# First norm taken from token rows, constants loaded between weight chunks, output turned by diagonal products and stored tile by tile

## The chip, the cores and the metric

One core of one Trainium2 chip runs the whole program. The metric is device time in microseconds (us) of one execution; the lower, the better. Engines: PE is TensorE, DVE is VectorE, ACT is ScalarE, POOL is GpSimd, SP is SyncE, which here only issues DMAs. Three runs of the kernel before gave 3411.03 us in the median (3408.16 to 3412.96).

## The reference

512 tokens of 1024 features, float32, pass two stacks of two layers each.

```python
def first_block(x, ...):
    for l in range(2):
        h = rmsnorm(x, mix_norm[l])
        p = h @ w_in[l]                       # 1440 columns
        a = mla_mixer(p..., positions, ...)   # 8 heads, with rotated positions
        b = pool_mixer(p..., w_pool[l], pool_scale[l])
        c = sg_mixer(p..., sg_norm[l], w_s[l], b_s[l])
        x = x + concat(a, b, c) @ w_o[l]
        h = rmsnorm(x, ffn_norm[l])
        x = x + (silu(h @ w_gate[l]) * (h @ w_up[l])) @ w_down[l]
    return rmsnorm(x, final_norm)

def second_block(x, c, ctx, c_ctx, ...):      # also 256 context tokens
    for l in range(2):
        sh1, sc1, g1, sh2, sc2, g2 = ada_params(c, ada_w[l], ada_b[l])
        y = mixer(rmsnorm_2(x, norm_g[l, 0]) * (1 + sc1) + sh1, ...)
        x = x + g1 * rmsnorm_2(y, norm_g[l, 1])
        h = rmsnorm_2(x, norm_g[l, 2]) * (1 + sc2) + sh2
        x = x + g2 * rmsnorm_2(swiglu(h, ...), norm_g[l, 3])
    return x
```

A norm divides each token's features by the root of the mean of their squares and multiplies them by a gain per feature.

## The kernel before

**Layout.** Activations lie transposed: xT is [128 features, 8 groups k, 512 tokens]. The input arrives as token rows (xin, four tiles of 128 tokens, 512 KB each) and PE turns it into xT by 32 transposes against an identity; the output is turned back in the same way (L3510), copied from PSUM to xout by ACT and DVE (L1400, L2499), and stored by one DMA (L645).

**Products in three parts.** A float32 matrix is split into a high part (rounded, "H") and the remainder ("L"), and each product is H·H + H·L + L·H. For a chunk c of weights, SP loads raw[c % 2] (L491), ACT makes WH (`hi(c)`, L728) once PE has used chunk c-2, and POOL makes WL (`low_parts`, L675). PE waits for WL (`chunk(c)`), SP for the WL of chunk c-2 before it loads over the raw buffer. A chunk of the first projection is 48 products of 512 columns.

**Norms.** ACT squares each group, the squares are added (by DVE, L1428, for the norms in ADDED; by PE, L2575, for the others), PE sums over partitions (L2587), ACT takes the root (L746), DVE the reciprocal (L1435), and PE spreads it over partitions with four products against the identity (L2603, `to_all`) into M[1]. Then, for each k, DVE makes ht = x · gain · M[1] (L1458), ACT rounds it to hH (L782, `rounded`), DVE makes hL = ht - hH (L1450), and PE multiplies as they come (`opening`, L2536). `rounded` lets ACT make one weight chunk's high part (`late`) after k = 1. In stages named in AWAKE, `keep_busy` sends products of the identity with itself into S[0] (L2565) where PE would idle; "b0.n1", the first norm, is not among them.

**Start.** Queues run in program order:

- SP: four tiles of x (L606), chunks 0 and 1, then `small_operands` (L547 to L555: 38 DMAs of constants, most of them 4 bytes for each element, all counted by the semaphore consts_loaded), then chunk 2 and the rest.
- ACT: `hi(0)`, `hi(1)`, half of the copies from PSUM to xT (L1086), the squares, the root, the rounding; then it waits for consts_loaded, takes Silu of cvec (L820), Exp of lbe (L822) and Sin for the rotation tables (L824), and goes on to the latents (L831) and `hi(2)`.
- DVE: the other half of the copies (L1744), the sums, the norm, then `once()`: the bounds (L1665 to L1681) and the angles (L1687 to L1703).
- PE: the 32 transposes, the norm's sums, chunks 0, 1, 2 and so on (`first_mixing`).

**End.** The last feed-forward adds its products to m_y (L1528). Then comes the norm "m.y2" and, in `added`, for each k: ht = m_y · gain · M[1] (L2074) and xT = xT + ht (L2081); then the transposes.

**The norm m.n2**, ahead of the last feed-forward, is one of those that PE sums (`column_sums`, L2575, with one product of `keep_busy` between two k).

## Time and profile before

| | |
|---|---|
| median of 3 runs | 3411.03 us (3408.16 to 3412.96) |
| the profiled execution | 3414.15 us, its span 3412.3 us |
| PE busy | 3179.8 us (93%) |
| DVE, ACT, POOL busy | 1898.6, 1149.3, 1242.3 us |
| chain that ended last, by engine | PE 77%, DVE 14%, ACT 4% |
| mean granted clock of PE | 0.957 |

The times inside the trace count from the start of the span. An engine's row "[11.17 <-POOL WL L675]" says that the engine sat idle for 11.17 us before this instruction, and that POOL's instruction of line 675 ended that. "x8" is the number of instructions merged; a float32 product against the identity or the ones counts as two matmul records, a transpose as one. PEclk is the granted clock of PE: 1.00 is 2.4 GHz, 0.50 is 1.2 GHz.

### The profile page before, as it was taken

The page shows a single profiled execution, that of the slowest core. Times are in us where ns is not written, and L with a number is a line of the kernel's source. Part 1 is how long each engine was busy: PE and PEld are TensorE (multiplying, and loading weights), DVE is VectorE, ACT ScalarE, POOL GpSimd, SP SyncE. Part 2 cuts the span into 40 slices and gives each one's busy share as a digit, 9 for nine tenths or more (in the row PEclk, how much of TensorE's full clock was granted, in tenths as well). Part 3 has the DMA queues.
Part 4 walks back from the last instruction along what each step waited for, and adds up shares of the span by engine and source line. Part 5 has one row for each costly group of instructions (what it writes and reads, how often), then busy time and mean ns, then how long its engine had stood idle before and what let it go on. Part 6 is the DMA issues. An engine that isn't in the chain of part 4 may idle for free.

```text
span 3412.3 us, 41861 instructions
## 1 busy us (share of the span) xinstructions
PE 3179.8 (93%) x16574; PEld 2612.2 (77%) x16574; DVE 1898.6 (56%) x3031; ACT 1149.3 (34%) x1801; POOL 1242.3 (36%) x556
## 2 busy tenths in 40 slices
PE   5888999998899999998999989889999999999997
PEld 4646788877469888777888988768888876788886
DVE  2753778766644454674434867558665437352224
ACT  3343222233435432324335544332223324432221
POOL 2301444533027543334344445124444330134442
PEclk8889999999899999998999989789999899999998
DMA  6201355533025332223333333125554220113331
GB/s 116 68 13 50 124 176 155 167 100 75 18 70 152 114 89 82 74 75 99 99 101 100 108 102 118 62 75 173 169 171 130 69 75 1 38 56 102 96 93 50
DMA packets 481716, 324.41 MB, mean 95 GB/s; under 512 B 103617, under 2 KB 448833, under 8 KB 481009
## 3 DMA queue, kind: packets, MB, share of 16 engines
q1 hardware_dynamic: 477056, 310.37, 30.9%
q10 hardware_dynamic: 2656, 6.30, 0.5%
q0 software_dynamic: 1808, 5.05, 0.5%
q8 instruction: 132, 2.16, 0.3%
q14 instruction: 64, 0.52, 0.0%
HBM read 316.41 MB, written 5.24 MB: 94 GB/s over the span
## 4 chain that ended last, share of the span: by engine, by line
PE 77%; DVE 14%; ACT 4%; issue 2%; SPq 2%; POOL 1%; DVEq 0%; DMA 0%; ACTq 0%
PE G L2511 11%; PE G L2520 11%; PE G L2521 11%; PE G L2525 11%; PE G L2695 5%; PE G L2696 5%; PE G L2700 5%; PE G L2536 2%; PE M L2875 2%; POOL WL L675 1%; PE S L2511 1%; PE M L2575 1%; ACT WH L728 1%; SPq L555 1%; DVE rstd L1428 1%
## 5 line engine op out<-in xcount | busy, mean ns | idle before, releaser
L675 POOL TENSOR_TENSOR WL<-raw,WH 128x1024 fp32r<-128x1024 f32 (+1 forms) x520 | 1225.5, 2379 | 2029.4 <-ACT WH L728 2029.4
L728 ACT ACTIVATE WH<-raw 128x1024 fp32r<-128x1024 f32 (+1 forms) x520 | 492.6, 995 | 625.4 <-PE G L2700 415.3
L2520 PE MATMUL G<-hH,WH 128*128 128x512 f32 x1520 | 595.6, 392 | 0.0
L2521 PE MATMUL G<-hL,WH 128*128 128x512 f32 x1520 | 592.8, 390 | 0.0
L2525 PE MATMUL G<-hH,WL 128*128 128x512 f32 x1520 | 360.1, 389 | 0.0
L2520 PEld LDWEIGHTS G<-hH,WH 128*128 128x128 f32 x1520 | 285.9, 188 | 60.2
L2521 PEld LDWEIGHTS G<-hL,WH 128*128 128x128 f32 x1520 | 285.9, 188 | 58.9
L2525 PEld LDWEIGHTS G<-hH,WL 128*128 128x128 f32 x1520 | 285.3, 188 | 59.3
L1491 DVE SCALAR_TENSOR_TENSOR acc<-adaw,cvec,acc 128x512 f32<-128x512 f32 x280 | 250.6, 947 | 4.2
L2511 PE MATMUL G<-hH,WH 128*128 128x512 f32 (+1 forms) x448 | 177.3, 396 | 29.5 <-POOL WL L675 26.9
L2511 PE MATMUL G<-hH,WL 128*128 128x512 f32 (+1 forms) x448 | 173.7, 388 | 0.0
L2511 PE MATMUL G<-hL,WH 128*128 128x512 f32 (+1 forms) x448 | 173.6, 388 | 0.0
L1515 DVE TENSOR_TENSOR FH<-silu,G 128x512 fp32r<-128x512 f32 x44 | 30.2, 687 | 215.6 <-PE G L2525 158.3
L2695 PE MATMUL G<-FH,WH 128*128 128x512 f32 x352 | 142.2, 404 | 0.2 <-DVE xT L1528 0.2
L2696 PE MATMUL G<-FL,WH 128*128 128x512 f32 x352 | 140.1, 398 | 0.0
L1428 DVE TENSOR_TENSOR rstd<-rstd,sq 128x512 f32<-128x512 f32 (+1 forms) x105 | 76.2, 725 | 104.0 <-ACT sq L763 96.8
L2511 PEld LDWEIGHTS G<-hH,WH 128*128 128x128 f32 x448 | 87.7, 196 | 48.5 <-POOL WL L675 28.2
L792 ACT ACTIVATE silu<-G 128x512 f32<-128x512 f32 x44 | 26.3, 598 | 273.2 <-PE G L2525 264.4
L1518 DVE TENSOR_TENSOR FL<-silu,FH 128x512 fp32r<-128x512 f32 x44 | 107.5, 2444 | 1.5
L1515 DVE TENSOR_TENSOR m_FH<-m_silu,G 128x512 fp32r<-128x512 f32 x22 | 15.1, 687 | 158.6 <-PE G L2525 156.3
L2511 PEld LDWEIGHTS G<-hL,WH 128*128 128x128 f32 x448 | 87.8, 196 | 16.5 <-issue 0.7
L2511 PEld LDWEIGHTS G<-hH,WL 128*128 128x128 f32 x448 | 87.4, 195 | 16.8
(659 smaller groups left out, 6338.0 us busy)
## 6 DMA issues: line engine op xcount, KB each, us to landing
raw<-ffn_w_in_in SPq DMA_DIRECT2D x264, 256.0 KB, 3.4
adaw<-ada_w_in SPq DMA_DIRECT2D x48, 1024.0 KB, 5.3
raw<-ab_w_in_in SPq DMA_DIRECT2D x128, 256.0 KB, 3.0
raw<-ffn_w_out_in SPq DMA_DIRECT2D x96, 256.0 KB, 2.9
raw<-w_gate_in SPq DMA_DIRECT2D x88, 256.0 KB, 3.4
raw<-w_up_in SPq DMA_DIRECT2D x88, 256.0 KB, 3.5
raw<-w_down_in SPq DMA_DIRECT2D x64, 256.0 KB, 2.8
raw<-w_in_in SPq DMA_DIRECT2D x40, 256.0 KB, 3.1
```

The lines of the kernel that those rows point to most:

```text
L675: nc.gpsimd.tensor_tensor(WL[c % 2][:, cut], raw[c % 2][:, cut], WH[c % 2][:, cut].bitcast(F32), ALU.subtract)\
L728: nc.scalar.activation(WH[c % 2][:, cut], raw[c % 2][:, cut], ACT.Copy).then_inc(weights_hi, 1)
L1428: V.tensor_tensor(rstd[:, 0:cols], rstd[:, 0:cols], sq[:, k % 2, 0:cols], ALU.add).then_inc(dve_done, did("dve", f"{n}.ad{k}"))
L1491: V.scalar_tensor_tensor(sums[:, b, i, :], weights[h % 2][:, k, :], col, sums[:, b, i, :], ALU.mult, ALU.add)\
L1518: V.tensor_tensor(FL[:, j, :], silu[:, t % 2, :], FH[:, j, :].bitcast(F32), ALU.subtract).then_inc(dve_done, did("dve", f"{n}.FL{t}"))
L2511: last = mm(dst, x, y, start=(k == 0 and j == 0), stop=(k == K - 1 and j == 2))
L2520: mm(dst, view(WH[c % 2], k), high, start=(k == 0 and not (joint and i)), stop=False)
L2521: mm(dst, view(WH[c % 2], k), low, start=False, stop=False)
L2525: last = mm(dst, view(WL[c % 2], k), X(k)[0], start=False, stop=(k == K - 1 and not (joint and i == 0)))
L2695: mm(dst, part(WH, k, cols, o), high, start=(k == 0 and not (joint and i)), stop=False)
L2696: mm(dst, part(WH, k, cols, o), low, start=False, stop=False)
L2700: last = mm(dst, part(WL, k, cols, o), X(k)[0], start=False, stop=(k == count - 1 and not (joint and i == 0)))
```

## The change

- The four tiles of x have a semaphore each. As each tile lands, ACT squares its token rows with the sum accumulated along the row (no sums on DVE or PE), and PE transposes its 8 blocks; ACT and DVE copy them to xT. The root is taken from the four sums; PE only spreads it. "b0.n1" joins AWAKE, and PE sends 8 products of the identity ahead of each tile.
- ACT makes `hi(0)` after the root and `hi(1)` as `late` in the rounding. PE starts the opening with half of chunk 0's low part.
- Six constants (rope_cols, posi, g_q, g_kv) are issued by ACT's queue. The others stand on SP's queue between chunks 1, 2, 3, 4 and 5, with three semaphores in place of one. `once()` is split: the angles stay behind the first norm, the bounds, Silu and Exp go behind the first attention.
- The norm m.n2 has, for each k, four transposes of xT in place of one `keep_busy` product; ACT copies them to xtok, in token rows.
- The tail: gdiag[k] = identity · gain (8 DVE instructions inside the last feed-forward). PE makes m_y (as left operand) times gdiag into eight half tiles in eight PSUM banks, and DVE adds each, times the token's 1/root, to xtok in one instruction. Each tile is stored as it is ready. The 16 DVE instructions of `added`, the spreading, and the eight copies to xout are gone.

```diff
-        CONSTS = 2 + 4 * DEPTH + 2 + 2 + 6 * DEPTH + 6 + 3 + 3
+        CONSTS = DEPTH + 1 + 2 + 6 * DEPTH + 6 + 3 + 3
+        TURNS = 2 + 2 * DEPTH
+        POOLING = 1 + DEPTH
...
                 if l == 0:
-                    small_operands()
+                    small_operands_0()
...
                 for n in range(3):
+                    if l == 0:
+                        (small_operands_1, small_operands_2, small_operands_3)[n]()
                     load(c + 3 + n, columns(c + 3 + n, w, r0 + ROPE + n * 2 * P))
...
-            sp.dma_start(out[0].rearrange("(t p) d -> p t d", p=P), xout[:, :, :]).then_inc(stored, 16)
+            for t in range(4):
+                sp.wait_ge(dve_done, at("dve", f"out.{t}1"))
+                sp.dma_start(out[0, t * P:t * P + P, :], xtok[:, t, :]).then_inc(stored, 16)
...
+            for t in range(4):
+                act.wait_ge(x_loaded[t], 16)
...
+                nc.scalar.activation(spare..., xin[:, t, :], ACT.Square, accum_out=rstd[:, t:t + 1])
+                act.wait_ge(pe_done, at("pe", f"x.{t}"))
+                nc.scalar.activation(xT[:, 0:4, t * P:t * P + P], G[2 * (t % 2)][:, :]..., ACT.Copy)
+            act.wait_ge(act_done, here())
+            nc.scalar.activation(rstd[:, 4:8], rstd[:, 0:4], ACT.Sqrt, bias=eps[:, 0:1], scale=1.0 / D)
             hi(0)
-            hi(1)
...
+            pe.wait_ge(early_loaded, 16)
+            for t in range(4):
+                keep_busy("b0.n1", 8)
+                pe.wait_ge(x_loaded[t], 16)
...
+                for k in range(KD):
+                    last = nc.tensor.transpose(G[2 * (t % 2) + k // 4][...], xin[:, t, k * P:k * P + P], ident[:, :])
+                last.then_inc(pe_done, did("pe", f"x.{t}"))
+            keep_busy("b0.n1", 8)
...
+            pe.wait_ge(dve_done, at("dve", f"gdiag{KD - 1}"))
+            for t in range(2):
+                out_blocks(t, range(KD - 2))
+            pe.wait_ge(dve_done, at("dve", f"m.down3.{KD - 1}"))
+            for t in range(2):
+                out_blocks(t, range(KD - 2, KD))
+            pe.wait_ge(dve_done, at("dve", f"m.y2.ad{KD - 1}"))
...
+            out_blocks(2, range(KD))
+            out_blocks(3, range(4))
+            pe.wait_ge(dve_done, at("dve", "m.y2.rec"))
+            out_blocks(3, range(4, KD))
```

SP's queue at the start, from chunk 1 on (raw_52 holds even chunks, raw_53 odd ones; every x counts DMAs). Before:

```order
L491 DMA raw_53<-w_in_in 128x2x256 x4
L547 DMA pool_inv<-tables_in 128x1024
L550 DMA g_ffn<-ffn_norm_in 128x8x1 x2
L552 DMA posi<-positions_in 128x512
L555 DMA ada_b<-ada_b_in 128x48x1 x2
L555 DMA g_n<-norm_g_in 128x8x1 x4
L555 DMA lbe<-hgrn_lb_in 128x4x1 x6
L555 DMA gate_b<-ab_gate_b_in 16x1
L491 DMA raw_52<-w_in_in 128x8x128
```

and in the change:

```order
L497 DMA raw_53<-w_in_in 128x2x256 x4
L549 DMA g_pool<-pool_scale_in 128x2x1 x2
L549 DMA g_ffn<-ffn_norm_in 128x8x1 x2
L497 DMA raw_52<-w_in_in 128x8x128 [waits weights_lo]
L565 DMA pool_inv<-tables_in 128x1024
L549 DMA ada_b<-ada_b_in 128x48x1 x2
L549 DMA lbe<-hgrn_lb_in 128x4x1 x6
L497 DMA raw_53<-w_in_in 128x2x256 [waits weights_lo]
L549 DMA g_n<-norm_g_in 128x8x1 x4
L497 DMA raw_52<-w_in_in 128x2x256 [waits weights_lo]
L549 DMA gate_b<-ab_gate_b_in 16x1
```

Of the 38 small DMAs that stood ahead of chunk 2, 7 still do; 9 now stand between chunks 2 and 3, 4 between 3 and 4, 12 between 4 and 5, and 6 are on ACT's queue.

PE at the start (S is the bank that `keep_busy` writes, M<-ident,ncol the spreading, L2536 and L2606 the opening). Before:

```order
L2887 MATMUL G<-ident,xin 128x128 x32
L2587 MATMUL M<-ones,rstd 128x1 x4
L2603 MATMUL M<-ident,ncol 128x128 x4
L2536 MATMUL G<-hH,WH_54 128x512
L2536 MATMUL G<-hL,WH_54 128x512
```

and in the change, where the first two rows come four times:

```order
L2637 MATMUL S<-ident 128x128 x8
L2980 MATMUL G<-ident,xin 128x128 x8
L2637 MATMUL S<-ident 128x128 x10
L2688 MATMUL M<-ident,ncol 128x128 x4
L2606 MATMUL G<-hH,WH_54 128x512
L2606 MATMUL G<-hL,WH_54 128x512
```

The sums over partitions are gone, and 42 products of the identity stand between the transposes and ahead of the spreading.

PE at the end, behind the last product of the feed-forward. Before:

```order
L2700 MATMUL G<-m_FH,WL_57 128x512 x8
L2565 MATMUL S<-ident 128x128 x8
L2587 MATMUL M<-ones,rstd 128x1 x4
L2565 MATMUL S<-ident 128x128 x2
L2603 MATMUL M<-ident,ncol 128x128 x4
L3510 MATMUL G<-ident,xT 128x128 x32
```

and in the change:

```order
L2785 MATMUL G<-m_FH,WL_57 128x512 x8
L3602 MATMUL G<-gdiag,m_y_244 128x128 x6
L3602 MATMUL S<-gdiag,m_y_244 128x128 x6
L3602 MATMUL S<-gdiag,m_y_244 128x128 x2
L3614 MATMUL M<-ones,rstd 128x1 x4
L3602 MATMUL M<-gdiag,m_y_244 128x128 x4
L3602 MATMUL G<-gdiag,m_y_244 128x128 x8
```

Sixteen of the 32 diagonal products stand ahead of the sums, and nothing is spread or transposed behind them.

## Rows read from the trace of the kernel before

**Rows 1.** Timeline of PE from the start: start us, us, instruction, count, idle before.

```profile
11.48 3.68 PE L2887 MATMUL G<-ident,xin 128*128 128x128 f32 x16 [11.48 <-DMA xin<-x_in]
...
32.73 2.08 PE L2603 MATMUL M<-ident,ncol 128*128 128x128 f32 x8 [0.55 <-DVE ncol L1435]
...
71.68 0.80 PE L2511 MATMUL G<-hH,WH 128*128 128x512 f32 x1 [11.17 <-POOL WL L675]
```

**Rows 2.** Timeline of SP's queue, DMA issues.

```profile
10.61 1.41 SPq L547 DMA_DIRECT2D pool_inv<-tables_in  x1
...
23.97 5.52 SPq L555 DMA_DIRECT2D ada_b<-ada_b_in  x2
29.54 6.37 SPq L555 DMA_DIRECT2D g_n<-norm_g_in  x4
...
47.23 4.56 SPq L555 DMA_DIRECT2D lbe<-hgrn_lb_in  x6
...
55.18 22.00 SPq L491 DMA_DIRECT2D raw<-w_in_in  x16
```

**Rows 3.** Timelines of DVE and POOL, end of the first norm and the angles.

```profile
44.60 1.48 DVE L1450 TENSOR_TENSOR hL<-ht,hH 128x512 fp32r<-128x512 f32 x2
...
59.68 0.42 DVE L1687 CAST posf<-posi 64x512 f32<-64x512 int32 x1
...
66.96 9.30 POOL L675 TENSOR_TENSOR WL<-raw,WH 128x1024 fp32r<-128x1024 f32 x4 [43.12 <-ACT WH L728]
```

**Rows 4.** Tile xin: landing. Tile ident: issue (ns, first and last start) and landing.

```profile
DMA to landing us min/median/max: 3.7/6.6/9.3
...
L652 POOL DMA_DIRECT2D ident<-tables_in x1: 679/679/679, 1.2 to 1.2; - x1
...
DMA to landing us min/median/max: 6.1/6.1/6.1
```

**Rows 5.** Timeline of PE around the norms of the last layer.

```profile
2984.48 1.95 PE L2565 MATMUL S<-ident 128*128 128x128 f32 x16
...
2998.58 1.71 PE L2575 MATMUL M<-ones,sq 128*128 128x1 f32 x8
...
3007.54 1.91 PE L2603 MATMUL M<-ident,ncol 128*128 128x128 f32 x8
```

**Rows 6.** Timelines of DVE and POOL in the norm b0.n2.

```profile
337.94 1.53 DVE L1458 SCALAR_TENSOR_TENSOR ht<-xT,g_ffn,M 128x512 f32<-128x512 f32 x2 [1.25 <-PE M L2603]
...
344.97 2.09 DVE L1450 TENSOR_TENSOR hL<-ht,hH 128x512 fp32r<-128x512 f32 x1
...
350.52 1.47 DVE L1450 TENSOR_TENSOR hL<-ht,hH 128x512 fp32r<-128x512 f32 x2
...
341.16 5.35 POOL L675 TENSOR_TENSOR WL<-raw,WH 128x1024 fp32r<-128x1024 f32 x2 [12.75 <-ACT WH L728]
```

**Rows 7.** A stretch of PE at full clock: us, PE busy (records), PEclk, DMA share, GB/s.

```profile
49.40:60.40 11.00, 11.00 (x50) 1.00 0.70 95
```

**Rows 8.** The chain that ended last, behind the wait at 71.68 us.

```profile
71.68 19.38 PE G L2511 x72
```

**Rows 9.** The output's transposes: weight loads in ns, and PE by stretch, as in rows 7.

```profile
L3510 PEld LDWEIGHTS G<-ident,xT x32: 139/144/230, 3399.3 to 3404.1; 128*128 128x128 f32 x32
...
3400.00:3402.00 2.00, 2.00 (x11) 0.50 0.03 8
3402.00:3404.00 2.00, 2.00 (x18) 0.97 0.00 0
```

**Rows 10.** Timelines of DVE and SP at the end.

```profile
3380.30 3.07 DVE L1428 TENSOR_TENSOR rstd<-rstd,sq 128x512 f32<-128x512 f32 x4
...
3387.20 0.75 DVE L2074 SCALAR_TENSOR_TENSOR ht<-m_y,mcols,M 128x512 f32<-128x512 f32 x1 [2.17 <-PE M L2603]
...
3398.53 0.69 DVE L2081 TENSOR_TENSOR xT<-xT,ht 128x512 f32<-128x512 f32 x1
...
3405.26 0.40 SPq L645 DMA_DIRECT2D out<-xout  x1
```

More of the change, by code:

```diff
@@ L1095, in _ @@
                     hi(c + 3)
+                    act.wait_ge(consts_loaded, 16 * CONSTS)
+                    nc.scalar.activation(cvec[:, :, :], cvec[:, :, :], ACT.Silu).then_inc(act_done, did("act", "cvec"))
+                    act.wait_ge(dve_done, at("dve", "lb.x"))
+                    nc.scalar.activation(lbe[:, :, :, :], lbe[:, :, :, :], ACT.Exp).then_inc(act_done, did("act", "lb.e"))
                     for k in range(4):
@@ L1397, in _ @@
             second_half(PM, xT)
-            for t in range(4):
-                act.wait_ge(pe_done, at("pe", f"out.{t}"))
-                nc.scalar.activation(xout[:, t, 0:512], G[2 * (t % 2)][:, :], ACT.Copy).then_inc(act_done, did("act", f"out.{t}"))
         @block.vector
@@ L2089, in second_half @@
                 feed_forward(n, ps.y2, N, ps.FH, ps.FL, ps.silu, fresh=True, between=between, last=f"{n}.y2")
-                added(n, 2, ps.y2, x, gain(p, 3), N)
+                if n == "m":
+                    added_sums("m.y2")
+                    roots("m.y2")
+                    for t in range(4):
+                        for half in range(2):
+                            dve.wait_ge(pe_done, at("pe", f"out.{t}{half}"))
+                            dve.wait_ge(dve_done, here())
+                            o = xtok[:, t, half * 512:half * 512 + 512]
+                            V.scalar_tensor_tensor(o, OUT[t][half][:, :], ncol[:, t:t + 1], o, ALU.mult, ALU.add).then_inc(dve_done, did("dve", f"out.{t}{half}"))
+                else:
+                    added(n, 2, ps.y2, x, gain(p, 3), N)
             def own(ins, name):
@@ L2495, in _, with last_gains @@
             added("m", 1, j_y, xT, gain("m", 1), T)
-            second_half(PM, xT, "m")
-            for t in range(4):
-                dve.wait_ge(pe_done, at("pe", f"out.{t}"))
-                V.tensor_copy(xout[:, t, 512:1024], G[2 * (t % 2) + 1][:, :]).then_inc(dve_done, did("dve", f"out.{t}"))
+            def last_gains():
+                for k in range(KD):
+                    yield
+                    V.tensor_scalar(gdiag[:, k, :], ident[:, :], gain("m", 3)(k), None, ALU.mult).then_inc(dve_done, did("dve", f"gdiag{k}"))
+            second_half(PM, xT, "m", last_gains())
         @block.tensor
@@ L2540, in came @@
             def came(n, k):
+                if n == "b0.n1" and k == KD // 2:
+                    pe.wait_ge(weights_lo, 2)
                 pe.wait_ge(act_done, at("act", f"{n}.H{k}"))
@@ L2588, in feature_sums @@
                     last.then_inc(pe_done, did("pe", f"{n}.sum"))
+                elif n == "m.n2":
+                    for k in range(K):
+                        pe.wait_ge(act_done, at("act", f"m.n2.sq{k}"))
+                        for t in range(4):
+                            last = mm(M[0][:, t:t + 1], sq[:, k % 2, t * P:t * P + P], ones[:, 0:1], start=(k == 0 and t == 0), stop=(k == K - 1 and t == 3))
+                        last.then_inc(pe_done, did("pe", f"m.n2.sq{k}"))
+                        if k == K - 1:
+                            tally.also("pe", "m.n2.sum")
+                        if k >= 4:
+                            pe.wait_ge(act_done, at("act", f"m.xt{k - 4}"))
+                        for t in range(4):
+                            last = nc.tensor.transpose(G[k % 4][:, t * P:t * P + P], xT[:, k, t * P:t * P + P], ident[:, :])
+                        last.then_inc(pe_done, did("pe", f"m.xt{k}"))
                 else:
```

168 lines of the change are left out of this document (105 added, 63 removed).

## The prediction

> **What bounds the kernel now.** The page comes first: PE is busy for 93% of the span and holds 77% of the chain that ended last, so a change pays only where PE stands still or runs at its low clock. The change touches three such places, so I read the timelines of the first 100 us, of the norm m.n2 and of the last 35 us.
>
> At the start, [rows 1] show PE beginning at 11.48 us, when the last tile of x has landed, and spreading the norm's roots from 32.73 to 34.81. The next thing to see is the idle time before 71.68: PE has done chunks 0 and 1 and waits 11.17 us for POOL's low part of chunk 2. That is no work of POOL's: its row in [rows 3] sat idle for 43.12 us before. Chunk 2 was issued only at 55.18 [rows 2], behind the small DMAs. At the end [rows 10] PE has nothing to do while DVE makes the norm's output from 3387.20 to 3399.22, and the store is issued at 3405.26, 7.04 us before the span ends.
>
> **The head.** PE now starts when the identity is there: issued at 1.2, landed 6.1 later [rows 4], 7.4 us. Its queue to the spreading: 4·8 + 10 = 42 products of the identity, 84 records at 0.12 (16 in 1.95, [rows 5]) is 10.1; 32 transposes at 0.144 (the median weight load of [rows 9], which paces them) is 4.6; the spreading, 8 records at 0.12, is 1.0. Its clock will be low at first: with dense short products it rose within about 3 us of the start in [rows 9], and 3.5 us at half speed cost 1.7. Sum: 7.4 + 10.1 + 4.6 + 1.0 + 1.7 = 24.8, against 34.81 before (32.73 + 2.08). The tiles are no bound: all had landed by 11.48 [rows 1], perhaps 2 us later now, since ACT's six constants share the DMA engines; PE wants the last at about 20. Nor is ACT: a tile takes PE 3.1 us, and a square of 1024 columns and a copy of 512 would be 2.3 even at DVE's 0.75 per 512 [rows 10]. So the products that keep PE awake are themselves the path here: the sums and the root would be ready 2 us sooner.
>
> The norm itself gets longer. Before, DVE took from 34.84 to 46.08 [rows 3], 11.2 us, with POOL idle. In b0.n2 the same eight steps ran from 337.94 to 351.99, 14.05 us [rows 6], since POOL made two low parts in that time (5.35 us): the hL at 344.97 took 2.09 where it takes 0.69, ending when POOL's first or second instruction ended. Each POOL instruction under the norm costs 1.4. Here ACT makes chunk 0's high part just ahead of the rounding and chunk 1's in it, so three or four of POOL's four instructions fall under the norm: three, 4.4 us, counting the first as over by the time hL begins. The Trainium skill (SBUF — State Buffer, "Who interferes with whom") says that a DVE instruction with two SBUF inputs and a GpSimd one that reads SBUF exclude each other for the whole instruction; by that rule the whole of this term stands and a kernel with POOL idle would have none, and rows 6 agree.
>
> DVE thus ends at 24.8 + 11.2 + 4.4 = 40.4, PE's opening 1.6 later (the six products of the last k, 1.4, and the hand-over), 42.0; chunk 1, 48 products, takes 10.9 at full clock (50 in 11.00, [rows 7]) and ends at 52.9. The weights of chunk 2 are by then just ready: SP loads it when chunk 0's low part is done, near 28, and it lands by 34; but ACT makes its high part behind the Sin, which waits for DVE's angles. From the first angle at 59.68 to the two low parts, 66.96 + 9.30/2 = 71.61, it was 11.9 before [rows 3]; now 40.4 + 11.9 = 52.3, against 52.9. PE begins chunk 2 near 53 where it did at 71.68: **18.7 us**.
>
> It also begins it at full clock. Before, PE had idled for 11 us, the clock was low (its first record took 0.80, [rows 1]), and 72 products took 19.38 [rows 8] instead of 72 · 0.227 = 16.3: **3.1 us**. The head gives 21.8.
>
> **What covers the constants.** SP issues chunk 2 by 31, then pool_inv, two ada_b and six lbe: these took 1.41, 5.52 and 4.56 us [rows 2], to 42.5; chunk 3 is issued by 46 and landed by 50, and ACT wants it at 53. Four g_n (6.4), chunk 4 by 55, wanted at 74; the last twelve (5.5 and 6.4 as before, six at lbe's 0.76, 16.5), chunk 5 by 74 and landed by 77, wanted at 86. The wanted times are those of before, shifted with PE. The nearest is 3 us from a wait. If that cover goes, PE waits by the difference. On ACT the Silu and Exp with their table loads, some 3 us, go into the output projection of the first layer, and DVE's second half of the bounds and the residual k = 2 queue behind them; PE wants that residual only three products' groups later, over 10 us. Nothing.
>
> **m.n2.** Before, PE's clock fell within the sums: those of a k took 1.71 where full clock makes it 1.0, and the spreading began at 3007.54 and took 1.91 [rows 5]. Now each k has four transposes (0.6, or 0.92 at low clock: 16 in 3.68, [rows 1]) instead of one product (0.2 to 0.5). If the clock stays up, PE keeps pace with DVE's 1.5 a k and spreads by 3004.6, at the high clock too: 3.4 less. If it falls as before, five k at 0.35 more and the last transposes: 2.4 more. These two are the bounds; nothing in the trace is nearer to either, so I take 0. The Trainium skill (TensorE: Matmul & The Clock Gate, "Part 4: PE-mode transpose") says that transposes do not bring PE to full clock; in [rows 9] it went from 0.50 to 0.97 within transposes alone, so I do not take it. By that rule the sum would be 2.4 us worse.
>
> **The tail.** The eight gdiag are small DVE instructions in a feed-forward where DVE idles 6.8 of 10.9 us a tile: nothing. PE waits for DVE's last addition, 3380.4, then does 16 diagonal products, 32 records at 0.12: 3384.3; the sums (1.0) 3385.3, the DVE sums that they want being done at 3383.4 [rows 10]. Root and reciprocal follow as before within 0.5: 3385.8. PE's other 32 records take 3.9, to 3389.3. DVE's eight instructions cost what L2074 does, 0.75 and a wait, 0.78: 6.2, to 3392.0, so DVE is the bound. The last store is 512 KB. From both sides: 7.04 as the 2 MB took [rows 10], or 3.7 as the quickest load of 512 KB [rows 4]; it is nearest to the load, with 0.4 to the span's end: 4.1. End at 3396.1, against 3412.3: **16.2 us**. At PE's low clock (records at 0.24) PE would be the bound, to 3398, and the gain 9.
>
> **Sum.** 18.7 + 3.1 + 0 + 16.2 = 38.0 from the profiled execution's own 3414.15 gives 3376.1. The median of the runs lies 3.1 below that execution, so I expect a median of **3373 us**. What a measurement of this kernel can tell from no change is about 0.2%, 6.8 us.
>
> **Rivals.**
> - *The warm-up stays cold.* PE's first products here are identity products and the clock might not rise for them. Then the spreading ends at 7.4 + 84·0.24 + 32·0.23 + 1.9 = 36.9, after the old 34.81 (records at the 1.91/8 of rows 5, transposes at the 3.68/16 of rows 1); the norm ends at 52, PE reaches chunk 2 at 64.5. The head gives 10 instead of 21.8: 3385. Against it: rows 9. 0.12.
> - *No POOL collisions, clock kept.* If POOL's work falls between DVE's, 4.4 is not paid, and with m.n2 at full clock 3.4 is won: 3365. For it: the first pair might be over before hL starts. 0.17.
> - *A new wait for a chunk.* The small DMAs, moved between chunks, take 1.8 times as long as alone, since weights share the engines: SP's three groups (11.5, 6.4, 16.5) end 27 us later, and chunk 5 comes some 18 late: 3391. For it: before, two issues of ada_b took 5.52, the four of g_n 6.37, so some of them block. 0.07.
> - *Slower.* The same mechanism at its far end. At chunk 5 the slack is 10 us and every unit of the factor r costs 34.4: the wait is 34.4(r - 1) - 10, and it exceeds the gain of 38 plus 6.8 from r = 2.6 on. At r = 3 the kernel takes 3373 + 58.8 = 3432. Against it: the 38 issues took from 10.61 to 55.18 all together [rows 2], and weights load the engines only for a few us a chunk. 0.02.
> - *The output's products do not hide.* The tail alone at low clock: 3380. 0.07.
>
> **Numbers.** My case has 0.55. The range 3361 to 3387 takes in m.n2's 3.4 and 2.4, the head within 5 either way, the store's 3, and the first, second and last rivals. Faster by over 0.2%: 0.97; within: 0.01; slower: 0.02.
>
> **What would show it.** PE's first record near 7.4, the spreading done near 25, three hL of over 1.6 us under POOL's instructions, chunk 2 started near 53 with no wait named after POOL and PEclk 1.00 from 50 to 90. ACT's wait for raw chunks zero behind 30 us. In m.n2, PEclk tells which bound holds. At the end, DVE's eight instructions back to back, the store issued some 12 us behind the last addition to m_y. I am wrong if PE waits for chunk 3, 4 or 5, if the spreading ends after 30, or if PE, not DVE, sets the pace of the tail.

## The result

The changed kernel takes **3376.55 us** as the median of four runs (3375.12 to 3381.25), the kernel before 3411.24 beside it (3408.16 to 3412.96): a ratio of 0.9898, 95% interval 0.9886 to 0.991. The forecast was 3373 in a range of 3361 to 3387. The profiled execution took 3381.25 us, the longest of the four; before, 3414.15.

The page of the changed kernel: its span and busy times, and the granted clock in 40 slices.

```profile
span 3379.3 us, 42066 instructions
...
PE 3187.0 (94%) x16688; PEld 2621.2 (78%) x16688; DVE 1900.5 (56%) x3016; ACT 1150.5 (34%) x1801; POOL 1242.8 (37%) x556
...
PEclk9899999998999999998999989789999899989999
```

The timeline of PE answers to [rows 1]: the first record and the transposes, the spreading, the opening.

```profile
7.13 3.78 PE L2637 MATMUL S<-ident 128*128 128x128 f32 x16 [7.13 <-DMA ident<-tables_in]
10.70 1.21 PE L2980 MATMUL G<-ident,xin 128*128 128x128 f32 x8
...
21.96 1.06 PE L2688 MATMUL M<-ident,ncol 128*128 128x128 f32 x8
...
27.26 0.47 PE L2606 MATMUL G<-hH,WH 128*128 128x512 f32 x1 [0.91 <-DVE hL L1495]
```

And the chain of waits from the norm's end on (start us, us, what). PE runs from the opening (L2606) through chunk 1, chunk 2 and the first half of chunk 3 (L2581, 120 products) without a pause, where before it waited 11.17 us for chunk 2.

```profile
32.84 8.55 PE G L2606 x36
41.39 27.20 PE G L2581 x120
```

SP's queue answers to [rows 2]: the chunks now stand between the small DMAs, and the same ada_b pair costs 5.16 us of a queue that nobody waits for.

```profile
24.27 4.64 SPq L497 DMA_DIRECT2D raw<-w_in_in  x4
...
30.08 5.16 SPq L549 DMA_DIRECT2D ada_b<-ada_b_in  x2
...
41.93 3.46 SPq L497 DMA_DIRECT2D raw<-w_in_in  x4
```

DVE in the first norm and, in the last line, POOL beside it, as in [rows 3, 6]: three hL of 2.1 to 2.6 us (two are shown, the third is like the second) under POOL's four low parts, then 0.69.

```profile
24.50 2.61 DVE L1495 TENSOR_TENSOR hL<-ht,hH 128x512 fp32r<-128x512 f32 x1
...
27.81 2.09 DVE L1495 TENSOR_TENSOR hL<-ht,hH 128x512 fp32r<-128x512 f32 x1
...
33.40 0.69 DVE L1495 TENSOR_TENSOR hL<-ht,hH 128x512 fp32r<-128x512 f32 x1
...
21.89 10.26 POOL L692 TENSOR_TENSOR WL<-raw,WH 128x1024 fp32r<-128x1024 f32 x4 [15.21 <-ACT WH L745]
```

The end, DVE and SP, as in [rows 10]: the sums behind the last addition to m_y, the first two and the last of the eight output instructions, and the four stores.

```profile
3364.19 3.07 DVE L1473 TENSOR_TENSOR rstd<-rstd,sq 128x512 f32<-128x512 f32 x4
...
3369.57 1.60 DVE L2155 SCALAR_TENSOR_TENSOR xtok<-G,ncol,xtok 128x512 f32<-128x512 f32 x2
...
3375.56 0.75 DVE L2155 SCALAR_TENSOR_TENSOR xtok<-M,ncol,xtok 128x512 f32<-128x512 f32 x1
...
3371.20 5.46 SPq L662 DMA_DIRECT2D out<-xtok  x4
```

**Where the time went.** A norm's spreading is one short instruction group at a fixed place in the program, so the same one in two traces, subtracted, says how far ahead the kernel is there. Rows of PE in the kernel before:

```profile
102.42 1.14 PE L2603 MATMUL M<-ident,ncol 128*128 128x128 f32 x8
...
1006.22 0.61 PE L2603 MATMUL M<-ident,ncol 128*128 128x128 f32 x4
...
2988.37 1.16 PE L2603 MATMUL M<-ident,ncol 128*128 128x128 f32 x8
```

and the same in the change:

```profile
79.95 1.14 PE L2688 MATMUL M<-ident,ncol 128*128 128x128 f32 x8
...
990.34 0.60 PE L2688 MATMUL M<-ident,ncol 128*128 128x128 f32 x4
...
2969.99 1.16 PE L2688 MATMUL M<-ident,ncol 128*128 128x128 f32 x8
2991.41 1.91 PE L2688 MATMUL M<-ident,ncol 128*128 128x128 f32 x8
```

The change is 22.47 us ahead after the head, 18.38 ahead before m.n2, 16.13 behind it (3007.54 in [rows 5] against 2991.41), and 33.0 at the end of the span. So the head gave 22.5, the middle took 4.1 back, m.n2 cost 2.25, and the tail gave 16.9. In the middle the change only moves the bounds, Silu and Exp, inside the first layer, and at the spreading of 336.75 us it is still 22.4 ahead: the loss comes later, in code that is the same in both kernels. Two of the four were open: whose fault the middle is, and why m.n2 costs what it does.

### The profile page after: what moved, and what is told of

Its sections match the earlier page's. It is cut to its first block, busy times and chain, and to the rows that moved or that the text cites. A ratio compares the mean times of both kernels' runs of the same rounds, so it can differ in the third digit from the quotient of the medians.

```text
span 3379.3 us, 42066 instructions
## 1 busy us (share of the span) xinstructions
PE 3187.0 (94%) x16688; PEld 2621.2 (78%) x16688; DVE 1900.5 (56%) x3016; ACT 1150.5 (34%) x1801; POOL 1242.8 (37%) x556
## 4 chain that ended last, share of the span: by engine, by line
PE 79%; DVE 13%; ACT 4%; issue 2%; POOL 1%; DMA 0%; DVEq 0%; ACTq 0%; POOLq 0%
PE G L2581 12%; PE G L2590 11%; PE G L2591 11%; PE G L2595 11%; PE G L2780 5%; PE G L2785 5%; PE G L2781 5%; PE G L2606 3%; PE M L2966 2%; POOL WL L692 1%; PE S L2581 1%; ACT WH L745 1%; PE M L2647 1%; PE S L2637 1%; DVE ht L1503 1%
## 5 line engine op out<-in xcount | busy, mean ns | idle before, releaser
L2581 PE MATMUL G<-hH,WH 128*128 128x512 f32 (+1 forms) x448 | 176.5, 394 | 18.3 <-POOL WL L692 15.7
L2581 PE MATMUL G<-hL,WH 128*128 128x512 f32 (+1 forms) x448 | 173.0, 386 | 0.0
L2581 PE MATMUL G<-hH,WL 128*128 128x512 f32 (+1 forms) x448 | 172.9, 386 | 0.0
L2581 PEld LDWEIGHTS G<-hH,WH 128*128 128x128 f32 x448 | 86.9, 194 | 36.8 <-POOL WL L692 16.7
L2581 PEld LDWEIGHTS G<-hL,WH 128*128 128x128 f32 x448 | 87.4, 195 | 16.4 <-issue 0.7
L2581 PEld LDWEIGHTS G<-hH,WL 128*128 128x128 f32 x448 | 87.1, 194 | 16.6
```

Source lines behind the costliest of these rows:

```text
L2581: last = mm(dst, x, y, start=(k == 0 and j == 0), stop=(k == K - 1 and j == 2))
```

## The experiments

Eleven kernels ran, in three groups, each group with its own runs of the kernel before. Their shifts against the profiled execution of the kernel before, made as above, are in one table, which the sections refer to ("head": the spreading that stood at 102.42 us; "to m.n2": the one at 2988.37; "m.n2": its cost, negative where it gains; "tail": from m.n2's spreading, 3007.54, to the span's end, against 404.76 before; all in us).

```
kernel             head    to m.n2   m.n2   tail   time
the change         -22.5    -18.4    +2.3   -16.9  3376.6 (median of 4)
the change again   -22.7    -25.8    +2.3   -16.8  3373.7 (one run)
head alone         -23.2    -24.0    -0.1    -0.2  3389.4 (4)
tail alone          -1.5     -5.4    +2.1   -16.8  3393.8 (4)
constants first    -10.2    -17.5    +2.0   -16.9  3387.2 (4)
few awake          -24.7    -25.3    +1.9   -16.9  3373.9 (one run)
ScalarE free       -26.1    -30.6    +2.0   -16.8  3369.6 (4)
GpSimd early       -25.8    -25.7    +2.0   -16.9  3373.7 (4)
one store          -23.2    -21.3    +1.8   -12.9  3381.7 (one run)
m.n2 awake         -23.0    -26.1    -1.8   -17.7  3368.5 (one run)
m.n2 twice         -23.6    -24.0    -1.4   -17.7  3371.0 (one run)
best               -28.9    -32.7    -1.8   -17.7  3363.3 (4)
```

One number of the table has to be read with care. Six of these kernels have the change's head, not edited (the change twice, head alone, one store, m.n2 awake, m.n2 twice), and their heads differ by up to 1.1 us (-22.5 to -23.6); tail alone has the head of before and stands at -1.5, not at 0. So a difference of about 1 us between two heads, each from one trace, tells nothing, and the head's 22.5 is itself good to 1 or 1.5 us. Part of it is one place: 24 products of chunk 3 took 7.20 us in the change and 5.56 in head alone, one store and m.n2 twice, where the clock did not fall.

### The two halves alone: head_only and tail_only

head_only is the change with the norm m.n2 and the end as they were; tail_only the reverse.

```diff
 # head_only, against the change
-                        for t in range(4):
-                            last = nc.tensor.transpose(G[k % 4][:, t * P:t * P + P], xT[:, k, t * P:t * P + P], ident[:, :])
...
-                            V.scalar_tensor_tensor(o, OUT[t][half][:, :], ncol[:, t:t + 1], o, ALU.mult, ALU.add).then_inc(dve_done, did("dve", f"out.{t}{half}"))
+                added(n, 2, ps.y2, x, gain(p, 3), N)
 # tail_only, against the change
-            for t in range(4):
-                keep_busy("b0.n1", 8)
-                pe.wait_ge(x_loaded[t], 16)
+            pe.wait_ge(x_loaded, 16 * 4)
...
-                        (small_operands_1, small_operands_2, small_operands_3)[n]()
```

> The head of the change alone: first norm from token rows, products that keep PE awake, constants between the chunks. m.n2 and the tail are as before. My theory: the head saves 22 us (the spreading at 79.95 us in the trace of the change against 102.42 before), so 3411.2 - 22.5 = 3389 in the median, and PE begins chunk 2 near 52 us. Rival: the change of phase costs something further on (in the one trace of the change 4 us of the head's gain were gone again before m.n2, where PE's clock was low for longer), and then this is a steady loss: 3393.

> m.n2 with four transposes a k and the tail with diagonal products and four stores, on the head of before. My theory: the tail saves 16.9 us and m.n2 costs 2.3, as the two traces stand to each other from the last addition to m_y and in m.n2: 3411.2 - 14.6 = 3396.6. Rival: m.n2's 2.3 was chance, since the clock gate can fall earlier or later, and here PE's clock stays at 1.00 through m.n2: 3391.

Measured: head_only 3389.44 us (3384.92 to 3389.84), ratio 0.994 (0.9925 to 0.9954); tail_only 3393.82 (3393.25 to 3395.41), ratio 0.9956 (0.994 to 0.9973); the kernel before beside them 3409.76. The head alone thus gives 20.3 us and the tail with m.n2 15.9, together 36.2, where the whole change gives 34.7: they add up within what the runs scatter. head_only came out at the theory's 3389, not at the rival's 3393: the 4 us lost in the middle are no steady loss of the change. In the table each half shows its own column, and tail_only 1.5 us of the head besides. tail_only came out between its two forecasts by time, but its trace decides for the theory: m.n2's clock fell in it too (+2.1), and the tail gave 16.8. It also gained 3.9 us in a middle that is word for word that of before. That is the first sign that the middle is not a property of a kernel.

### Which part of the head: consts_first

The head with its new start, but all small constants ahead of chunk 2 again:

```diff
                 if l == 0:
-                    small_operands_0()
+                    for small in (small_operands_0, small_operands_1, small_operands_2, small_operands_3):
+                        small()
...
-                    if l == 0:
-                        (small_operands_1, small_operands_2, small_operands_3)[n]()
```

> The change with SP's 32 small DMAs all ahead of chunk 2 again, nothing else undone (the six on ACT's queue stay there, and ACT and DVE do not wait for the constants before the first attention). If the order of the constants is what keeps PE fed, SP issues chunk 2 only at 52 to 55 us (21.1 plus the 31 to 34 that the three groups took), the low part is ready at 63 to 66 where PE wants it at 52, and PE comes back at low clock: 12 to 17 us slower than the change, 3389 to 3394. Rival: the constants were never the bound, since the first norm started early is what moved everything: within 3 us of the change.

Measured: 3387.2 us (3381.82 to 3387.66), ratio 0.9932 (0.9918 to 0.9947), 10.7 above the change, a little under the 12 to 17 of the theory; by the trace the head is 12.2 us worse (-10.2 against -22.5). SP's queue, ACT and PE in that kernel:

```profile
51.60 15.58 SPq L497 DMA_DIRECT2D raw<-w_in_in  x16
...
55.81 1.06 ACT L744 ACTIVATE WH<-raw 128x1024 fp32r<-128x1024 f32 x1 [9.90 <-DMA raw<-w_in_in]
...
61.65 0.79 PE L2580 MATMUL G<-hH,WH 128*128 128x512 f32 x1 [8.65 <-POOL WL L691]
```

The old chain is back, one link after the other: chunk 2 issued at 51.60, ACT 9.90 us without it, PE 8.65 without the low part, and a record of 0.79 us where it starts again, the low clock. So 12.2 of the head's 22.5 us (within the 1 us by which heads differ) belong to the place of chunk 2 among the constants: PE starts it 9.4 us later than in the change (61.65 against 52.3), and the rest is the clock that is lost in the wait. The 10.2 that remain are not PE's earlier start either, or PE would not stand for 8.65 us at the end of it. SP issues chunk 2 at 51.60 instead of 55.18, since six constants, which took 5.7 us of its queue before, are ACT's now: 3.6. And Silu, Exp and the bounds, which had waited for the last constant, no longer stand ahead of the angles (59.68, [rows 3]): these are long done, so that ACT's high part follows 4.2 us behind the issue (55.81), where before it began at 65.83, 10.6 behind: 6.4. ACT in the kernel before:

```profile
65.83 2.00 ACT L728 ACTIVATE WH<-raw 128x1024 fp32r<-128x1024 f32 x2
```

The early start pays only once chunk 2 is early too. The reverse, constants between the chunks with the old start, was not tried.

### What paces the start: few_awake, act_free

The forecast called the products that keep PE awake the path of the start. few_awake sends 8 ahead of tile 0 and one ahead of the spreading, none between:

```diff
-                keep_busy("b0.n1", 8)
+                keep_busy("b0.n1", 8 if t == 0 else 0)
...
-            keep_busy("b0.n1", 8)
+            keep_busy("b0.n1", 1)
```

> The change with 8 products to keep PE awake ahead of the first tile only, none ahead of tiles 2 to 4, and 1 + 2 ahead of the spreading in place of 8 + 2. Theory: these products are on the path in the head; without them PE is done with the transposes by 16 us, and ACT is the bound, whose six DMAs held it until 11.4 us: its last copy ends near 19, and the spreading starts near 20.3 instead of 21.96, at full clock: 1.5 us gained. Rival: they pay for themselves, PE's clock falls without them and the opening's first products take 0.4 us each: the spreading as late as 22 or more, and no gain at chunk 2.

Measured: 3373.94 us; the spreading starts at 19.76 instead of 21.96, and the head is 2.3 us better. The warm-up was the path, as forecast, but only just. The rival was right that the clock falls without it: the 16 records of the identity product ahead of the opening took 3.78 us, against 2.05 in the change. It cost nothing, since PE made up for it behind DVE's steps: the opening ended 2.2 us earlier all the same. The next bound in that trace is ACT. Its timeline in the change shows why: it issues the six constants that the change gave it, one after the other, before it may square anything.

```profile
1.87 2.50 ACTq L1093 DMA_DIRECT2D rope_cols<-tables_in  x1
...
5.30 3.48 ACTq L1097 DMA_DIRECT2D g_q<-q_norm_in  x2
...
11.39 1.28 ACT L1099 ACT_TABLE_LOAD   x1 [11.39 <-issue]
```

That is 9.5 us of an engine for six small DMAs, with tile 0 long landed. act_free is few_awake with these six on SP's queue, behind chunk 1:

```diff
+                c0, n = a["at"]["rope_cols"]
+                sp.dma_start(rope_cols[:, :], a["tables"][:, c0:c0 + n]).then_inc(turns_loaded, 16)
...
-            act.dma_start(rope_cols[:, :], a["tables"][:, c0:c0 + n]).then_inc(turns_loaded, 16)
```

> One eighth of the products of identity before the transposes and one after tile 3 (as in the kernel with few of them), and the six element-wise constants that ScalarE issued ahead of its first square (11.39 us in the changed kernel) go to the SyncE queue behind chunk 1. Theory (the head was bound by ScalarE's own DMA issues once the products were few): ScalarE's first square comes when tile 0 lands, near 5 us, the spreading comes at 15.5 to 17 against 21.96, the span is 4 to 6 us shorter than the changed kernel's, median 3371. Rival 1: the six issues, some 9.5 us, now stand on the SyncE queue ahead of chunks 2 to 4, chunk 2 or 3 lands late and PE waits for it: 2 to 5 us given back, median 3375. Rival 2: with fewer products ahead the clock stays at half for the norm's start, worth 1 to 2 us.

Measured: 3369.6 us (3368.69 to 3371.0), ratio 0.9877 (0.9863 to 0.9892), 7 us below the change. The time is near the forecast, the reason is not: the spreading came at 18.44, not at 15.5 to 17, and the head is 3.6 us better than the change's, not 4 to 6. The rest of the 7 us is not in the head; in the two profiled executions the difference beyond it lies in the middle (below). ACT in that kernel:

```profile
4.54 1.06 ACT L1105 ACTIVATE sq<-xin 128x1024 f32<-128x1024 f32 x1 [1.06 <-DMA xin<-x_in]
...
12.68 0.60 ACT L1108 ACTIVATE xT<-G 128x512 f32<-128x512 f32 x1 [7.00 <-PE G L2980]
13.18 1.05 ACT L1105 ACTIVATE ht<-xin 128x1024 f32<-128x1024 f32 x1
```

The first square is done at 5.7, and then ACT stands for 7.00 us in front of the *copy* of tile 0, which waits for PE, while the square of tile 1 stands behind it in the same queue and needs nothing from PE. A free engine is not enough; its program order held it. PE did not wait for chunk 2 or 3, so rival 1 is out: SP's queue had room for six more. Rival 2 was right on the clock and wrong on the price. PE in act_free, ahead of the opening:

```profile
21.61 3.78 PE L2637 MATMUL S<-ident 128*128 128x128 f32 x16 [2.01 <-POOL WL L698]
...
30.64 0.47 PE L2606 MATMUL G<-hH,WH 128*128 128x512 f32 x1 [0.56 <-DVE hL L1495]
```

By the 3.78 us of these records the clock was low until about 26 us, but by 30.64 PE waited for DVE again, so nothing of it was left.

### GpSimd beside the norm: hi0_early

act_free, with ACT's high part of chunk 0, and so POOL's two low parts, ahead of the last tile:

```diff
+                if t == 2:
+                    hi(0)
...
-            hi(0)
```

> The kernel with ScalarE free, and GpSimd's work on the first norm's first tile issued inside the loop over the tiles, ahead of the norm's products. Theory (three steps of the norm on VectorE take 2.1 us instead of 1.0 each where GpSimd works beside them): GpSimd has done part of its work before VectorE starts, one or two of the three steps take 1.0 us, and the norm ends 1 to 2 us earlier than in the kernel with ScalarE free: 1.5 us less. Rival: GpSimd's work isn't ready to start earlier, since it needs the tile that VectorE copies last, and all stays as it was: 0.

Measured: 3373.68 us (3366.56 to 3383.42), ratio 0.9892 (0.9866 to 0.9917). Its four runs scatter over 17 us, so the 4 us above act_free are not shown to be the edit's. No gain in the head, -25.8 against -26.1; but not for the rival's reason. POOL in act_free, then POOL and PE in hi0_early:

```profile
19.21 10.73 POOL L698 TENSOR_TENSOR WL<-raw,WH 128x1024 fp32r<-128x1024 f32 x4 [12.54 <-ACT WH L751]
```

```profile
16.52 4.65 POOL L698 TENSOR_TENSOR WL<-raw,WH 128x1024 fp32r<-128x1024 f32 x2 [9.87 <-ACT WH L751]
24.82 5.37 POOL L698 TENSOR_TENSOR WL<-raw,WH 128x1024 fp32r<-128x1024 f32 x2 [3.65 <-ACT WH L751]
...
19.50 2.07 PE L2689 MATMUL M<-ident,ncol 128*128 128x128 f32 x8 [3.70 <-DVE ncol L1594]
```

POOL's first pair does end before DVE's norm begins at 21.61, and the norm on DVE takes 14.1 us (21.61 to 35.69) instead of 15.8 (19.64 to 35.44). Against the 11.2 with POOL idle ([rows 3], from 34.84) that is 2.9 with two collisions (0.3 of it a wait for ACT) and 4.6 with three (a fourth POOL instruction only brushed an hL, which took 1.02): 1.4 to 1.5 for each, the forecast's price. But the norm began 2 us later. ACT's 2 us for the high part stood ahead of the square of tile 3, so that the root came 1.1 us later than in act_free (18.93 against 17.88); and PE, idle for 3.70 us until then, made the spreading at the low clock, 2.07 us instead of 1.16. A collision was bought off at its own price. The Trainium skill (SBUF — State Buffer, "Who interferes with whom") gives the rule, an exclusive lock for the whole instruction between a DVE instruction with two SBUF inputs and a GpSimd one that reads SBUF; both traces agree with it: only hL, which has two such inputs, gets longer, and ht, with one operand in PSUM, takes 0.75 throughout.

### The norm m.n2: mn2_awake and mn2_twice

In every trace with the change's m.n2 the clock fell there and the stage cost 1.8 to 2.3 us. The timeline of PE in the change where it happens:

```profile
2974.89 1.05 PE L2665 MATMUL M<-ones,sq 128*128 128x1 f32 x8
2975.81 0.63 PE L2672 MATMUL G<-ident,xT 128*128 128x128 f32 x4
...
2977.41 1.09 PE L2672 MATMUL G<-ident,xT 128*128 128x128 f32 x4
2978.29 1.71 PE L2665 MATMUL M<-ones,sq 128*128 128x1 f32 x8
```

Four transposes go from 0.63 to 1.09 us and the sums from 1.05 to 1.71: the same instructions at 1.2 instead of 2.4 GHz. Either it is the transposes, for which by the Trainium skill the full clock does not engage (TensorE: Matmul & The Clock Gate, "Part 4: PE-mode transpose"), or the short pauses, in which PE waits for the next square. mn2_awake puts products into the pauses:

```diff
                     for k in range(K):
+                        if k:
+                            keep_busy(n, 2)
                         pe.wait_ge(act_done, at("act", f"m.n2.sq{k}"))
```

> The change with two rounds of products of identity ahead of each column group's sums in the multilayer part's second norm. In the changed kernel TensorE's granted clock fell to 0.50 there, near 2978 us, and the stage took 2.25 us more than in the kernel before. Theory (products hold the clock where transposes did not): the clock stays at 1.00 from 2976 to 2996, the shift of this norm's end against the kernel before grows from 16.1 to 17.5 to 20 us; span 3376 to 3378. Rival: the clock falls all the same, and the added products come on top: span 3381 to 3383.

Measured: 3368.53 us, and m.n2 gains 1.8 us instead of costing 2.3; that is 4.0 us, at the upper end of the forecast's 1.4 to 3.9, and most of the rest by which the time beats the forecast lies in the middle. That shows the cure but not the cause, since products and filled pauses came together. mn2_twice fills the pauses with transposes alone, each issued twice into the same place:

```diff
-                        for t in range(4):
+                        for t in (0, 1, 2, 3) * 2:
                             last = nc.tensor.transpose(G[k % 4][:, t * P:t * P + P], xT[:, k, t * P:t * P + P], ident[:, :])
```

> The change with every transpose in the multilayer part's second norm issued twice, into the same place, so that TensorE has as much more to do for each column group as with two products of identity, but of transposes alone. Theory A (transposes do not keep the clock up, whatever the engine's idle time): the clock falls to 0.50 near 2978 us all the same and the stage costs 2 us or more, since the added transposes come on top. Theory B (idle time between the groups let the clock fall): it stays at 1.00 and the stage gains 1 to 2 us against the kernel before, as with the products.

Measured: 3370.96 us, the clock stayed, m.n2 gained 1.4, as by theory B. The windows of the change (us, PE busy, PEld, DVE, ACT, POOL, PEclk, DMA share, GB/s):

```profile
2972.00:2978.00 6.00, 5.47 (x44) 4.97 (x43) 5.73 (x8) 3.16 (x6) 0.00 (x0) 0.94 0.01 3
2978.00:2984.00 6.00, 6.00 (x32) 6.00 (x30) 5.01 (x7) 3.88 (x7) 0.00 (x0) 0.50 0.00 0
```

and of mn2_twice:

```profile
2972.00:2978.00 6.00, 6.00 (x58) 6.00 (x58) 5.31 (x8) 4.51 (x9) 0.00 (x0) 1.00 0.00 0
2978.00:2984.00 6.00, 6.00 (x58) 6.00 (x57) 0.97 (x3) 2.20 (x6) 0.00 (x0) 1.00 0.02 4
```

At the same time mn2_twice stands 5.7 us further on in the program; over its whole norm, from 2969.59 to the spreading at 2982.08, each group of sums takes 0.95 us and never 1.71. PE does twice the transposes and is through sooner. What let the clock fall were the pauses: filled with transposes, which left sums and transposes back to back, they no longer did; and in [rows 9] transposes alone had raised the clock. Here the measurement and the Trainium skill's sentence differ, and the measurement decides. mn2_twice is one execution, but the clock fell in m.n2 in all ten traces that have the pauses (eight with the change's m.n2, two with the old one) and in none of the three that fill them. The kernel before lost its clock in this norm too, with one product and the same kind of pause for each k [rows 5].

The tail column shows one more thing. Where the clock was kept, the part behind the spreading is also 0.8 us shorter, since the spreading itself takes 1.06 us instead of 1.91. The whole price of the lost clock is thus 2.3 + 1.8 + 0.8 = 4.9 us.

### The store by tiles: one_store

```diff
-            for t in range(4):
-                sp.wait_ge(dve_done, at("dve", f"out.{t}1"))
-                sp.dma_start(out[0, t * P:t * P + P, :], xtok[:, t, :]).then_inc(stored, 16)
-            sp.wait_ge(stored, 16 * 4)
+            sp.wait_ge(dve_done, at("dve", "out.31"))
+            sp.dma_start(out[0].rearrange("(t p) d -> p t d", p=P), xtok[:, :, :]).then_inc(stored, 16)
+            sp.wait_ge(stored, 16)
```

> The change with one store of the whole output after the last of the eight steps on VectorE, instead of one for each tile. Theory: the store starts when the last step ends, and takes the 7.04 us that it took in the kernel before; the change's last tile's store took some 3 us behind the last step, so the span is 3 to 4.5 us longer, near 3383. Rival (the storing by tiles is hidden or bound by the transfers themselves): less than 1 us.

Measured: 3381.71 us, and 4.0 us of the tail gone (-12.9 against -16.9), within the theory. Its landing beside that of a tile's store in the change:

```profile
DMA to landing us min/median/max: 6.6/6.6/6.6
```

```profile
DMA to landing us min/median/max: 2.6/2.6/2.6
```

The landings differ by 4.0 us, which is the whole loss. So of the tail's 16.9 us, 4.0 are the four stores, 12.9 the work taken from DVE and PE.

### Is the middle the change's: after_again

The changed kernel once more, not edited.

> The change itself once more, unedited, for its profile. In the profiled execution of the changed kernel TensorE lost 2.4 us between 711 and 770 us and 3.4 us between 770 and 990 us against the kernel before, at a low clock, in code that the change does not touch. Theory (which of these stretches falls to the low clock differs from one execution to the next): in this profile one of the two is missing or others are there, and the time follows by that much, 3375 to 3382. Rival (the change's shift in time moves a phase, and the loss is the change's own): both losses again, within 0.5 us.

Measured: 3373.72 us, 1.3 under the theory's range; both losses are missing, not one of them. Its spreadings, to be set beside the ones above:

```profile
79.69 1.14 PE L2688 MATMUL M<-ident,ncol 128*128 128x128 f32 x8
...
979.92 0.60 PE L2688 MATMUL M<-ident,ncol 128*128 128x128 f32 x4
...
2962.55 1.16 PE L2688 MATMUL M<-ident,ncol 128*128 128x128 f32 x8
```

It is 22.7 ahead after the head and 26.3 ahead at the spreading that stands at 1006 us in the kernel before, where the first profile was 15.9 ahead: the same program, 10.4 us apart in the middle. A window of the first profile and the same place in this one, 3.55 us earlier:

```profile
711.00:730.00 19.00, 17.42 (x76) 14.73 (x77) 13.57 (x17) 6.99 (x11) 5.37 (x2) 0.83 0.19 56
```

```profile
707.45:726.45 19.00, 16.11 (x83) 12.69 (x83) 13.55 (x17) 8.09 (x14) 5.34 (x2) 1.00 0.18 56
```

A norm of the second layer ran at a granted clock of 0.83 in one execution and at 1.00 in the other. The kernel before has the like: between 114 and 337 us its profiled execution lost 3 to 4 us that seven of the twelve others did not (the change again went from -22.7 to -26.0 there, tail_only from -1.5 to -5.4, with a granted clock of 0.94 against 0.92 before). Both losses of the first profile do come back together in one other kernel, hi0_early (-25.8, and -19.4 at 1006), so they are a recurring pattern and not noise of every size; but the same kernel has them in one execution and not in the other, so the change alone does not make them. What decides it in an execution stays open.

### Both findings together: best

act_free, with ACT's four squares and the root ahead of its four copies, and mn2_awake's two products.

```diff
                     .then_inc(act_done, did("act", f"b0.n1.sq{t}"))
-                act.wait_ge(pe_done, at("pe", f"x.{t}"))
...
             nc.scalar.activation(rstd[:, 4:8], rstd[:, 0:4], ACT.Sqrt, bias=eps[:, 0:1], scale=1.0 / D).then_inc(act_done, did("act", "b0.n1.root"))
             root_before[0] = "b0.n1.bc"
+            for t in range(4):
+                act.wait_ge(pe_done, at("pe", f"x.{t}"))
```

> The kernel with ScalarE free, plus two edits. ScalarE makes the four squares and the root before its four copies of transposed tiles (before: square and copy by turns), and each column group's sums of the multilayer part's second norm have two products of identity ahead of them. Theory: the squares are done by 10.5 us and no longer stand between copies, the last copy ends near 16.5 instead of 17.8, DVE's first step of the norm starts at 17 instead of 19.64: 2.6 us. The clock stays at 1.00 in the second norm of the multilayer part: 3.8 us (its stage cost 2.03 there and gained 1.78 with those products). Median 3362 to 3365, against 3369.6. Rival 1 (TensorE's clock, low again after its first burst, or GpSimd's low parts eat the head's gain): 3.8 alone, median 3366. Rival 2 (what keeps TensorE awake in one execution is chance): no gain over the kernel with ScalarE free.

Measured: **3363.26 us** (3360.05 to 3370.17), ratio to the kernel before 0.9867 (0.9848 to 0.9886), 13 us below the change. ACT's squares now follow the tiles as they land, and the root (11.91) waits for no copy. The last of the four squares:

```profile
10.73 1.06 ACT L1105 ACTIVATE ht<-xin 128x1024 f32<-128x1024 f32 x1 [0.94 <-DMA xin<-x_in]
```

The spreading starts at 15.60, DVE's norm at 16.79 (19.64 in act_free, forecast 17), and the head is 2.8 us better, forecast 2.6. m.n2 keeps its clock. Both parts of the theory hold, each by its own column; for the head this is two single traces, each good to about 1 us. The norm itself still takes 15.8 us, with three collisions.

## Why the prediction was right, and where not

The profiled execution came out at 3381.25 where the sum said 3376.1; the median at 3376.55 where it said 3373. The 5 us between sum and profiled execution are 4.1 of the middle and 2.25 of m.n2, less 0.7 each by which head and tail were better than forecast; that these partly cancel is luck. By the sum's own terms:

- **PE starts at 7.4, spreading done at 24.8.** 7.13 and 23.03. The start was cold, as said: the first 16 records took 3.78 us instead of 1.95, which is 1.8 against the 1.7 of the sum. The 1.8 us too much are in the lengths of small things: a tile's eight transposes take 0.87, or 0.109 each, not 0.144, which was a weight load at mixed clock, and a record of the identity product 0.112, not 0.12. That the warm-up products are the path held: few_awake gained 2.3. The root was ready 1.1 us ahead of PE, though, not 2.
- **ACT is no bound.** Right by a hair, for a reason that the prediction did not have. It counted ACT's squares and copies, and not the 9.5 us that ACT's own six DMA issues hold its queue, though its own rows of SP's queue showed that such issues cost 1.6 to 2.8 us each ([rows 2]: 6.37 for four, 5.52 for two). The engine was ready with the root at 20.86, and PE with its warm-up at 21.96.
- **Three collisions of 1.4 us.** Three, of 1.9, 1.4 and 1.4; the norm took 15.97 us, forecast 15.6. Over the whole norm, the runs with two and three of them give 1.4 to 1.5 each.
- **Chunk 2 at 53, no wait for POOL.** The chain gives 41.39 for the opening's end and 27.20 for 120 products, so 0.227 each, and chunk 2 begins at 52.3. That is 19.4 earlier than before, forecast 18.7; with the clock kept, 22.5 against 21.8. consts_first removed the reason and the wait came back. One sign did not hold: PEclk was to be 1.00 from 50 to 90, and behind the sums at 68.59 it fell, in the change as it had before (24 products in 7.20 us in both), so it cancels in the sum:

```profile
72.00:76.00 4.00, 4.00 (x13) 3.13 (x12) 0.00 (x0) 2.62 (x4) 2.24 (x1) 0.57 0.01 2
```

- **Constants between the chunks are free.** No chunk was waited for. The prediction put chunk 3 at 46 and chunk 4 at 55; they were issued by 45.4 and 52.0, chunk 5 by 68.9 instead of 74. Even six more small DMAs did no harm.
- **m.n2: 0.** The step that failed. It took the middle between two bounds, clock kept (-3.4) and clock lost (+2.4), and gave as the reason that nothing was nearer. Measured: +2.25 and +2.27 in two executions of the change, and +1.8 to +2.1 in six more kernels with its m.n2, so this was never a toss-up. The bounds themselves were good: with the clock kept, 1.8 were gained in m.n2 and 0.8 behind it, 2.6 against the bound's 3.4. The evidence against 0 was in the trace: the kernel before had lost its clock in that very norm, with PE waiting for each square, and four transposes of 0.63 us do not fill that wait. The Trainium skill's rule would have given the right number, 2.4, for the wrong cause, which mn2_twice shows.
- **The tail: 16.2.** 16.9. DVE's eight instructions take 6.7 us instead of 6.2, a pair 0.86 apart and not 0.78; PE was never their bound. From the last store to the span's end the sum had 4.1 us, a load's 3.7 and 0.4; it took 3.0.
- **The middle: nothing.** The sum is made against one execution of before, which had lost 3 to 4 us, and the change's profiled execution had lost more: it ended 7.4 us behind its own repeat. In the medians this mostly cancels: head, m.n2 and tail make 37.1, and the medians differ by 34.7. The remaining 2.4 us are within what the runs of the change scatter (3373.7 to 3381.3), and are not explained further. The sum put this term at nothing without naming it.

## What to carry to other kernels

- A DMA issue costs the issuing engine its time, and a small strided one can cost more than a large block (2.6 us for one ada_b, 0.9 for one DMA of chunk 3). Ask of every queue what stands behind the issues: on SP it was a weight chunk, on ACT the first square of the kernel. On an engine that executes in order, put the work that needs nobody ahead of the work that waits.
- Where TensorE's clock is at stake, look for short pauses and try to fill them; here it mattered little with what. Some 0.5 us of useless products for each step made the stage 4 us shorter. This holds only where the engine waits anyway: at the start the same kind of products cost about 2 us and bought nothing.
- Compare stages by a marker at a fixed place in both traces, and take a second profile of the unedited kernel before explaining a difference in code that was not touched.

## What was unexpected of the hardware

- Transposes count for TensorE's clock as products do: in a stretch of short sums and transposes, with each transpose issued twice, PEclk stayed 1.00 from 2972 to 2984 us where it had fallen to 0.50.
- Six small DMAs on ScalarE's queue took 9.5 us of ScalarE (0.87 to 3.48 us a row), and its first instruction of arithmetic began at 12.69 us.
- Two executions of the same program lay 10.4 us apart after some 980 us, through stretches at a lower granted clock, and 7.4 us apart at the end.
- DVE's output instructions, each on one PSUM bank, follow one another after 0.86 us though one takes 0.75 (each waits for the end of the one before).
